# Retention in a hybrid decoder trunk: query and decayed query in one buffer, key and decayed key in another, two transpositions a chunk for three

## What is computed

```
# RET_HEADS = 4, dk = 64, dv = 128, chunks of C = 128 tokens, nc = 8
scores = jnp.einsum('bhncd,bhnkd->bhnck', qc, kc) * decay[None, :, None]
o_inner = jnp.einsum('bhnck,bhnkv->bhncv', scores, vc)
xi = jnp.exp(log_gamma[:, None] * (i + 1.0))
zeta = jnp.exp(log_gamma[:, None] * (C - 1.0 - i))
kz = kc * zeta[None, :, None, :, None]

def step(R, inp):
    q_n, kz_n, v_n = inp
    o = jnp.einsum('bhcd,bhdv->bhcv', q_n, R)
    R = R * chunk_decay[None, :, None, None] + jnp.einsum('bhcd,bhcv->bhdv', kz_n, v_n)
    return R, o
# o_cross * xi; retention = o_inner + o_cross, then a group norm, a gain and silu(gate)
```

## Time and profile before

| | |
|---|---|
| median of 3 runs | 2614.23 us (2612.29 to 2614.32) |
| the profiled execution | 2612.44 us, span 2610.7 us |
| mean granted TensorE clock | 0.981 of full |
| TensorE busy | 2486.2 us, 95% of the span |
| VectorE, ScalarE, GpSimd busy | 1075.7, 739.6, 806.7 us |
| chain that ended last, by engine | PE 84%, DVE 8%, POOL 3%, ACT 2%, issue 2% |

### The profile page before, as it was taken

The page is one execution under the profiler, slowest core; times in us unless marked ns, Lnnn a source line. Parts: engine busy times, 40 slices in busy tenths (PEclk is TensorE's granted clock), DMA queues, the critical chain, the costliest instruction groups (busy, mean ns, idle before and its releaser), DMA issues.

```text
span 2610.7 us, 34016 instructions
## 1 busy us (share of the span) xinstructions
PE 2486.2 (95%) x12520; PEld 2080.3 (80%) x12520; DVE 1075.7 (41%) x2591; ACT 739.6 (28%) x1487; POOL 806.7 (31%) x770
## 2 busy tenths in 40 slices
PE   5999999998989999999999799999989999999998
PEld 4787878787968888888887688879978888888886
DVE  7464645454323232323233566662322323232323
ACT  4424343331221212121221355552312121212220
POOL 4223132310333333333332233331133333333331
PEclk9999999998999999999999899998999999999999
DMA  3000000002211111111111200003011111111111
GB/s 115 25 25 25 25 25 25 25 19 80 69 33 49 48 48 48 48 48 48 48 48 43 89 26 25 25 25 103 31 49 49 48 48 48 48 48 48 48 48 65
DMA packets 108200, 120.20 MB, mean 46 GB/s; under 512 B 26048, under 2 KB 94144, under 8 KB 108096
## 3 DMA queue, kind: packets, MB, share of 16 engines
q1 hardware_dynamic: 100720, 103.70, 12.8%
q10 hardware_dynamic: 7376, 15.12, 1.7%
HBM read 110.41 MB, written 8.39 MB: 46 GB/s over the span
## 4 chain that ended last, share of the span: by engine, by line
PE 84%; DVE 8%; POOL 3%; ACT 2%; issue 2%; DMA 0%; POOLq 0%; SPq 0%; ACTq 0%; DVEq 0%
PE gp L350 11%; PE gp L352 10%; PE gp L351 10%; PE sc L350 5%; PE sc L352 4%; PE sc L351 4%; PE tp L351 4%; PE tp L352 4%; PE tp L350 4%; PE o_ps L434 4%; PE sc L400 3%; PE tp L422 2%; PE o_ps L350 2%; PE qt L350 2%; PE qt L351 2%; PE o_ps L352 2%
## 5 line engine op out<-in xcount | busy, mean ns | idle before, releaser
L1209 POOL TENSOR_TENSOR W_lo<-raw,W_hi 128x1024 fp32r<-128x1024 f32 (+2 forms) x200 | 433.7, 2183 | 704.1 <-ACT W_hi L620 704.0
L350 PE MATMUL gp<-W_hi,hT_hi 128*128 128x384 f32 (+1 forms) x1152 | 421.9, 366 | 14.8 <-POOL W_lo L1209 6.7
L352 PE MATMUL gp<-W_hi,hT_lo 128*128 128x384 f32 (+1 forms) x1152 | 384.3, 334 | 0.0
L351 PE MATMUL gp<-W_lo,hT_hi 128*128 128x384 f32 (+1 forms) x1152 | 383.9, 333 | 0.0
L620 ACT ACTIVATE W_hi<-raw 128x1024 fp32r<-128x1024 f32 (+2 forms) x200 | 186.4, 964 | 646.7 <-PE qt L352 559.0
L1148 DVE TENSOR_TENSOR r<-r 128x512 f32<-128x512 f32 x128 | 92.2, 720 | 626.8 <-ACT r L773 626.8
L1295 POOL TENSOR_TENSOR a_lo<-r,a_hi 128x512 fp32r<-128x512 f32 x128 | 166.0, 1298 | 447.5 <-ACT a_hi L775 447.5
L1155 DVE TENSOR_TENSOR X<-tp,X 128x512 f32<-128x512 f32 x256 | 176.8, 692 | 173.8 <-PE tp L352 171.7
L350 PEld LDWEIGHTS gp<-W_hi,hT_hi 128*128 128x128 f32 x1152 | 221.2, 192 | 26.9 <-issue 11.2
L351 PEld LDWEIGHTS gp<-W_lo,hT_hi 128*128 128x128 f32 x1152 | 221.6, 192 | 0.0
L352 PEld LDWEIGHTS gp<-W_hi,hT_lo 128*128 128x128 f32 x1152 | 219.9, 191 | 0.0
(11 more groups left out here) (187 smaller groups left out, 4083.8 us busy)
## 6 DMA issues: line engine op xcount, KB each, us to landing
raw<-in_mlp_w_up SPq DMA_DIRECT2D x64, 512.0 KB, 3.8
raw<-in_mlp_w_down SPq DMA_DIRECT2D x64, 512.0 KB, 3.2
raw<-in_hyb_w_in SPq DMA_DIRECT2D x80, 128.0 KB, 2.5
X<-in_x SPq DMA_DIRECT2D x8, 512.0 KB, 12.0
X<-in_x ACTq DMA_DIRECT2D x8, 512.0 KB, 3.2
raw<-in_swa_w_qkv SPq DMA_DIRECT2D x16, 256.0 KB, 2.7
x_spill<-X ACTq DMA_DIRECT2D x8, 512.0 KB, 2.6
X<-x_spill ACTq DMA_DIRECT2D x8, 512.0 KB, 3.3
```

The costliest lines, as they stand in the source:

```text
L350: mm(o, a[0], b[0], start=first, stop=False)
L351: mm(o, a[0], b[1], start=False, stop=False)
L352: return mm(o, a[1], b[0], start=False, stop=last)
L1209: E.tensor_tensor(W_lo[:, slot, c], raw[:, p % 2, 0:n], W_hi[:, slot, c].bitcast(f32), ALU.subtract).then_inc(w_ready, 1)
```

## The change

`rQK` becomes `rQ`, whose columns 0 to 63 are q and 64 to 127 are q times xi; k and k times zeta stand side by side in `QK`, columns 256 to 383. Each of the two is transposed as one 128 x 128 block, so q lands on partitions 0 to 63 and q times xi on 64 to 127 of `rqT[:, 0]`, k on partitions 0 to 63 of `rqT[:, 1]` (and k times zeta, unused, on 64 to 127). The product for the state takes the 128 columns k, k times zeta as its stationary operand, so that the part that is wanted comes out on partitions 64 to 127 of `r_add` (0 to 63 get a product with k that nobody reads). The state `rR` is kept on partitions 64 to 127. VectorE writes the rotated q and the rotated k by two instructions, since they go to two buffers.

```diff
-        rR = at("rR", [HD, 2, RV])
+        rR = at("rR", [P, 2, RV])
...
-        rQK = at("rQK", [P, 2, 2 * HD])
-        rqT = at("rqT", [HD, 3, P])
+        rQ = at("rQ", [P, 2, 2 * HD])
+        rqT = at("rqT", [P, 2, P])
...
-        r_add = sc[0:HD, P:P + RV]
+        r_add = sc[:, P:P + RV]
...
-                q, k, qx = rQK[:, r % 2, 0:HD], rQK[:, r % 2, HD:2 * HD], QK[:, r % 2, 4 * HD:5 * HD]
-                for m, src in enumerate((q, k, qx)):
-                    last = nc.tensor.transpose(qt[0:HD, m * P:(m + 1) * P], src, ident[:, :])
+                for m, src in enumerate((rQ[:, r % 2, :], QK[:, r % 2, 4 * HD:6 * HD])):
+                    last = nc.tensor.transpose(qt[:, m * P:(m + 1) * P], src, ident[:, :])
...
-                mm(sc[:, 0:P], rqT[:, 1, :], rqT[:, 0, :], start=True, stop=True)
-                mm(r_add, QK[:, r % 2, 5 * HD:6 * HD], v, start=True, stop=True).then_inc(r_st, 1)
+                mm(sc[:, 0:P], rqT[0:HD, 1, :], rqT[0:HD, 0, :], start=True, stop=True)
+                mm(r_add, QK[:, r % 2, 4 * HD:6 * HD], v, start=True, stop=True).then_inc(r_st, 1)
...
-                    last = mm(o, rqT[:, 2, :], rR[:, r % 2, :], start=False, stop=True)
+                    last = mm(o, rqT[HD:P, 0, :], rR[HD:P, r % 2, :], start=False, stop=True)
...
-                A(rqT[:, :, :].rearrange("p m c -> p (m c)"), qt[0:HD, 0:3 * P], ACT.Copy).then_inc(r_qtev, 1)
+                A(rqT[:, :, :].rearrange("p m c -> p (m c)"), qt[:, 0:2 * P], ACT.Copy).then_inc(r_qtev, 1)
...
-                q = rQK[:, r % 2, :]
-                step.did(E.tensor_tensor(q, rA, rB, ALU.add))
-                step.wait()
-
-                step.did(E.tensor_scalar(QK[:, r % 2, 4 * HD:5 * HD], q[:, 0:HD], xi[:, bass.ds(h, 1)], None, ALU.mult))
-                E.tensor_scalar(QK[:, r % 2, 5 * HD:6 * HD], q[:, HD:2 * HD], zeta[:, bass.ds(h, 1)], None,
+                q, k = rQ[:, r % 2, :], QK[:, r % 2, 4 * HD:6 * HD]
+                step.did(E.tensor_tensor(q[:, 0:HD], rA[:, 0:HD], rB[:, 0:HD], ALU.add))
+                step.did(E.tensor_tensor(k[:, 0:HD], rA[:, HD:2 * HD], rB[:, HD:2 * HD], ALU.add))
+                step.wait()
+
+                step.did(E.tensor_scalar(q[:, HD:2 * HD], q[:, 0:HD], xi[:, bass.ds(h, 1)], None, ALU.mult))
+                E.tensor_scalar(k[:, HD:2 * HD], k[:, 0:HD], zeta[:, bass.ds(h, 1)], None,
                                 ALU.mult).then_inc(r_qk, 1)
...
-                new = rR[:, (r + 1) % 2, :]
+                new = rR[HD:P, (r + 1) % 2, :]
                 if r == 0:
-                    E.tensor_copy(new, r_add).then_inc(r_R, 1)
+                    E.tensor_copy(new, r_add[HD:P, :]).then_inc(r_R, 1)
                 else:
                     dve.wait_ge(r_R, n)
-                    E.scalar_tensor_tensor(new, rR[:, r % 2, :], cdec[0:HD, bass.ds(h, 1)], r_add,
+                    E.scalar_tensor_tensor(new, rR[HD:P, r % 2, :], cdec[HD:P, bass.ds(h, 1)], r_add[HD:P, :],
                                            ALU.mult, ALU.add).then_inc(r_R, 1)
```

## The result

The change made the kernel slower: 2620.03 us median of 16 runs (2612.5 to 2624.5) against 2613.27 us (2610.4 to 2616.03) before, a ratio of 1.0026 with a 95% interval of 1.0018 to 1.0034. Forecast were 2612.9 us, a range of 2609.8 to 2616.5, and "no difference". The profiled execution took 2620.01 us, for 2612.44 before.

The account below looks back on a forecast made before the run. TensorE was taken as the bound, except where VectorE and GpSimd set the pace. Groups 0 to 2 gain 0.46 us each (1.38), the last loses 0.04: 2614.2 - 1.3 = 2612.9 us, range 2609.8 to 2616.5.

Parts of the forecast that it names:

- Rows 64 to 127: TensorE's L469 works on the upper rows; scores on either half take 0.48 and 0.49 us, so no cost.
- The pieces: Each 16-slot group cut up: two stretches bound by VectorE and GpSimd, chunks 5 to 7 by TensorE, then the unchanged seam.
- The transpositions: TensorE, two transpositions for three before L351: 0.40 us for 0.50, 0.10 gained in chunks 0, 5, 6, 7 of a group.
- (b): TensorE's stream resumes sooner behind the 128-column L459: 0.50 us to L351 for 0.64, 0.14 gained in chunks 5 to 7.
- (a): The 128-column state product L459 ends 0.06 us later, delaying VectorE's `rsT` twice a group.
- Two additions: VectorE's rotation adds two halves separately: 0.38 us for 0.32, 0.06 lost per rotation, four times a group.
- The seam: Stretch between groups, from the values of chunk 7: no changed work, the same 3.2 us wait of TensorE.
- Rival 2: VectorE's second addition does not overlap and costs the whole 0.32 us on 17 rotations: 2617.3 us; chance 0.08.
- Rivals 1 and 3: 1: TensorE's saving counts in full, 2606.8, chance 0.06; 3: only weight load counts, (b) nothing or less, 2614.9, chance 0.15.
- the case to which 0.04 was given: Something that the profile rows do not show, taken as a loss; chance 0.04.
- Rival 4: The clock falls otherwise at the phase's end, 604 to 620 us: perhaps 1 to 2 us either way; no chance given.

Follow-up runs that it names:

- swapped halves: The changed kernel with state and its update on rows 0 to 63, scores on rows 64 to 127: 2611.99 us, ratio 0.9995 to the kernel before.
- second profile: The changed kernel run once more, unedited, against the kernel before: 2618.76 us, ratio 1.0022.

## Why the prediction was wrong

**The step that failed** is the sentence "The state's update reads as many columns as before. Both at nothing.", with the part "Rows 64 to 127" ahead of it, which asked only TensorE what the upper rows cost. On VectorE they cost about 0.11 us at three places of a chunk (two in the first chunks of a group), 0.35 us of a period of 6.90. The swapped halves take it back entirely: 60.53 to 59.07 us a group, and 1.0022 to 0.9995 in time, 6.8 us. What the text weighed for VectorE was the number and size of instructions; what decided was whether the second of two could start before the first had ended.

This is a rule of the Trainium skill, VectorE: DVE Perf Modes, section "Two Vector instructions with no wait between them": an instruction is held until all earlier ones have finished if one of its inputs or its output starts in another quadrant of 32 partitions than the last read or write of the same memory, SBUF and PSUM apart. The prediction had not weighed it. The traces agree in each case: L987 (from row 0 to row 64), the instruction behind it where that touches SBUF (back to row 0), and L992, the next reader of PSUM, with eleven instructions between them that touch SBUF alone. It also says why L992 overlaps in chunks 1 and 2 of the changed kernel (gaps of -0.08 us) and not in the others: there L1066, which reads `o_ps` from row 0, stands between. In every late case here a read starts on other rows; whether an output alone would do it, no run shows.

**What bounds the kernel.** The pieces were right for the kernel before, and were what made the loss count: against it, A-B grew by 0.33 us and C-D by 0.79, the two stretches that hold TensorE's waits for VectorE. D-E shrank by 0.09 where the swapped halves shrink it by 0.62: there the late starts took back 0.53 of what TensorE had gained, 0.37 in the first period (7.34 us for 6.97) and 0.16 in chunks 5 to 7. Those the prediction took as bound by TensorE, which they no longer are: TensorE could go through them in 6.11 us, as with the halves swapped, and VectorE holds it to 6.17. That TensorE waits there was one of the prediction's signs of being wrong, and it does, by some 0.06 us a chunk, between the two instructions of L465. TensorE's wait before the values of chunk 4 rose from 0.30 to 0.96 us; forecast was 0.3 more.

**The transpositions**: 0.40 us as forecast. **The wide product (b)**: 0.50 us to L351 as forecast; the experiment with it alone gives 0.42 us for three chunks. **(a)**: its second instruction starts 0.21 us behind the first for 0.16, as B-C also shows (3.11 for 3.05), for 0.06 forecast; of the two loads that the prediction's estimate of 53 ns was for, one is seen (0.05 us). **Two additions**: 0.08 a rotation in the rows, 0.07 in the experiment, for 0.06. **The seam** kept its 3.2 us of wait; E-F grew by 0.05. With the halves swapped, these terms alone are left: a group gains 0.33 us for the 0.46 forecast, and the interval of the ratio, 0.9986 to 1.0004, holds the forecast's 1.3 us.

**Rival 2** had the right place, VectorE's rotation and what stands around it, and the right sign, but put the price on the second addition; its threshold of 0.14 us a rotation was far exceeded (0.45 in the period of chunks 2 and 3), by another cause. **Rivals 1 and 3** did not occur. What occurred is the case to which 0.04 was given, something that the rows do not show, taken as a loss. **Rival 4**: the clock took part. A longer wait before the attention values can put the stretch behind it at half clock. The estimate without it is 5.7 us, and the medians differ by 6.8 us in the first comparison and by 5.1 in the second, so by these numbers its share in the median is at most about 1 us; it was not measured by itself. In single executions it is more: in the first profile half clock behind the wait stands in all four groups, and makes two of them 0.8 us and two 1.9 us longer than groups without it in the second profile. The changed kernel's runs spread over 12 us for 6 before. How much of that spread is this wait and how much other stretches stays open. (The profiled execution also has half clock from 23.6 to 47.3 us, ahead of any changed instruction, which the profile before has not. So has the profile of the change once more, and its first state product is 0.3 us earlier than before, so that stretch is not where the time went.)

## What to carry to other kernels

Count, on an engine that sets the pace, not only instructions and columns but which neighbours overlap; a buffer that moves to other start partitions can take that overlap from its neighbours, even from one that comes much later and shares only the memory. Of two layouts that serve TensorE equally, take the one in which VectorE's operands start on the rows that everything around them starts on. And where a TensorE product on 64 rows or to 64 columns stands among full ones, filling it up with unused or zero data can be cheaper than the narrow shape (0.14 and 0.38 us a product here).

## What the runs showed of the hardware

- Two VectorE instructions with no wait between them: the second starts 0.08 us before the end of the first, but 0.03 us after it where it reads from row 64 and the last read of the same memory was from row 0. So 0.11 us are lost, the same on the way back, for PSUM and SBUF separately. It is so in all 32 chunks of the change (profiled twice) and of the kernels with PSUM or the state on upper rows, and in none of the other kernels.
- TensorE: from the state product to L351 0.64 us with 64 columns of weights and 0.50 with 128; the values' two products and the way to L351 1.00 us with the second on 64 rows and 0.62 on 128. The Trainium skill, TensorEngine Tiling (Array Packing), Key Properties, says that a change of tiling mode drains the engine, and gives no price; these rows agree that leaving and entering the narrow shape costs time, but part of it lies within the narrow product itself (0.48 us on 64 rows, 0.39 on 128), and transpositions of 64 columns do not pay it (0.10 us for the third).
- TensorE at half clock (0.50, 1.2 GHz) behind an idle of only 1.1 to 1.5 us, in some groups and executions and not in others of the same kernel: 16 of 36 such places, and none of 12 at 0.8 to 1.02 us.
